# Paired attention of the second block: three pairs of score banks, one value product per pair of heads, and coefficients spread inside the steps

## The reference, cut to what matters

```python
def nsa_mixer(q, kc_raw, vc_raw, ks, vs, kw, vw, gates, ...):   # 8 heads of 64, 2 groups of keys and values
    # compressed keys:  o_c = softmax(q kc) vc
    # selected blocks:  the top 8 blocks of 64 keys; 512 tokens have 8 blocks, so all are taken
    s_s = q k_sel^T ; p_s = masked_softmax(s_s, causal) ; o_s = p_s v_sel
    # window of 512 keys: with 512 tokens this is again every key up to the token's own
    s_w = q k_win^T ; p_w = masked_softmax(s_w, causal) ; o_w = p_w v_win
    o = gates[0] * o_c + gates[1] * o_s + gates[2] * o_w
...
    return concatenate([o_a, o_b, o_c], axis=-1) @ w_out     # attention, pooling, gated linear attention
```

## Time and profile before

| what | us |
|---|---|
| median of 3 runs (3054.70 to 3055.62) | 3055.57 |
| the profiled execution, device time | 3055.25 |
| its span in the trace | 3053.4 |
| PE busy | 2989.9 |
| DVE busy | 1881.9 |
| ACT busy | 1284.5 |
| GpSimd busy | 1082.1 |
| attention of the second block, first layer, from the first turn to the first output product | 1558.21 to 1634.77 |
| the same, second layer | 2551.34 to 2627.90 |

### The profile page before, as it was taken

How to read it: one execution, slowest core, us unless ns; L and a number is a source line. 1 busy time by engine, 2 the same in 40 slices (tenths; PEclk the granted TensorE clock), 3 DMA queues, 4 the chain that set the end, 5 groups by cost and what they waited for, 6 DMA issues and landing times. The chain is left out here.

```text
span 3053.4 us, 43808 instructions
## 1 busy us (share of the span) xinstructions
PE 2989.9 (98%) x17636; PEld 2517.3 (82%) x17636; DVE 1881.9 (62%) x2718; ACT 1284.5 (42%) x2007; POOL 1082.1 (35%) x794
## 2 busy tenths in 40 slices
PE   8999999999999999999999999999999999999998
PEld 6887878788777789987867899978998776789996
DVE  7476244837524277854475777657785447577774
ACT  4356442436553243433473534324343347453432
POOL 2443445525354422325341332242232534133222
PEclk8999999999999999999999999999999999999999
DMA  6223315313231233222210233223322221033321
GB/s 272 100 84 110 100 43 200 138 59 111 97 104 53 83 114 104 94 90 80 81 42 29 104 104 104 97 76 114 104 95 89 77 83 42 29 104 104 104 97 49
DMA packets 57441, 287.63 MB, mean 94 GB/s; under 512 B 6776, under 2 KB 7288, under 8 KB 30200
## 3 DMA queue, kind: packets, MB, share of 16 engines
q1 hardware_dynamic: 54000, 269.30, 25.0%
q10 hardware_dynamic: 3240, 15.53, 1.6%
HBM read 282.64 MB, written 2.16 MB: 93 GB/s over the span
## 5 line engine op out<-in xcount | busy, mean ns | idle before, releaser
L152 POOL TENSOR_TENSOR w_parts<-w_raw,w_parts 128x512 fp32r<-128x512 f32 x376 | 535.7, 1456 | 717.3 <-ACT w_parts L141 691.9
L421 PE MATMUL PS<-x_parts,w_parts 128*128 128x512 f32 x2688 | 667.9, 394 | 1.6 <-ACT m_all L1424 1.6
L421 PEld LDWEIGHTS PS<-x_parts,w_parts 128*128 128x128 f32 x2688 | 500.5, 188 | 113.2 <-issue 9.6
L2169 POOL TENSOR_TENSOR partial_parts<-ffn_buffers,partial_parts 128x512 fp32r<-128x512 f32 x128 | 184.3, 1441 | 746.9 <-ACT partial_parts L2364 746.9
L2210 PE MATMUL PS<-hidden_parts,partial_parts 128*128 128x512 f32 x1536 | 372.7, 391 | 0.0
L2210 PEld LDWEIGHTS PS<-hidden_parts,partial_parts 128*128 128x128 f32 x1536 | 280.1, 188 | 53.4
L2190 PE MATMUL PS<-x_parts,w_parts 128*128 128x512 f32 x1152 | 264.8, 390 | 1.0 <-POOL x_parts L873 0.8
L2190 PEld LDWEIGHTS PS<-x_parts,w_parts 128*128 128x128 f32 x1152 | 215.3, 188 | 50.4 <-POOL x_parts L873 1.8
L141 ACT CAST w_parts<-w_raw 128x2048 fp32r<-128x2048 f32 (+1 forms) x92 | 170.6, 1855 | 158.8 <-PE PS L421 73.8
L2228 PE MATMUL PS<-x_combined_parts,w_parts 128*128 128x256 f32 x1536 | 204.2, 282 | 0.2
L2228 PE MATMUL PS<-x_parts,w_parts 128*128 128x256 f32 x1536 | 204.2, 282 | 0.0
(11 more groups left out here) (442 smaller groups left out, 5002.4 us busy)
## 6 DMA issues: line engine op xcount, KB each, us to landing
w_raw<-in_w_gu SPq DMA_DIRECT2D x88, 1024.0 KB, 4.8
w_raw<-in_w_in SPq DMA_DIRECT2D x70, 1024.0 KB, 4.9
ffn_buffers<-in_w_part SPq DMA_DIRECT2D x128, 256.0 KB, 2.7
w_raw<-in_w_out SPq DMA_DIRECT2D x24, 1024.0 KB, 4.8
m_all<-in_w_next SPq DMA_DIRECT2D x14, 1024.0 KB, 7.4
w_raw<-in_w_last SPq DMA_DIRECT2D x12, 768.0 KB, 4.2
m_all<-in_w_gate SPq DMA_DIRECT2D x8, 1024.0 KB, 4.8
ssd_buffers<-decay_rows ACTq DMA_DIRECT2D x16, 512.0 KB, 3.8
```

The lines of the kernel that those rows point to most:

```text
L152: pool.tensor_tensor(self.part(parts, u, 1, at, to), raw[:, self.slot(u), at:to], self.part(parts, u, 0, at, to).bitcast(F32), ALU.subtrac ...
L421: return pe.matmul(PS[0:m, self.bank(j), :], w[w_][:, k, c:c + m], part(x_, k), start=start, stop=stop)
L2169: pool.tensor_tensor(small_parts[:, d % 2, 1, :], small_raw[:, d % 2, :], small_parts[:, d % 2, 0, :].bitcast(F32), ALU.subtract).then_inc ...
```

## The change

The score of a step and its transposes now share a bank: step s uses banks 2(s % 3) and 2(s % 3) + 1, so three steps are under way in banks 0 to 5. turn(s, b) writes over the scores of step s, which DVE has read. score(s) therefore waits until both copies of step s - 3 are done, where it waited for the maximum of step s - 2. The PE list of a step becomes turn(s, 0), score(s + 2), `between(s)`, turn(s, 1), and after turn(3n + 3, 1) the weigh of the whole pair n. That weigh is eight products (four key tiles by two heads) with 512, 384, 256 and 128 columns instead of twenty with 128. The pt buffer holds a whole pair, laid out by key tile (`turned_tile`), so the copies of step 3n + 2 are two instructions each. Odd pairs' pt lies in the two slots of `RAW`; copy(3) waits until unit 11 has been split, and SP sends units 12 and 13 only after the last weigh.

Coefficients are computed per pair of heads in DVE's `after` of steps 2, 5, 8, ...; they are spread in `between` of steps 8, 10, 12, 14, 16, 19 and 22, all into bank 7, and scaled by DVE a step later. The finish of the gated linear attention is done in every second step from 0 to 14. Tiles 4 to 7 are rounded with pairs 1, 2, 3 and 5. The last pair's weigh and spread go into `proj.begin`, ahead of its n = 2; tiles 0 to 2 are rounded ahead of the last `take_output`.

```diff
             def begin(self, pe, jobs, x, order=range(KD), between=None):
                 for n in range(KD + 1):
+                    if between and n in between:
+                        between[n]()
...
+            def bank(self, s, b):
+                return 2 * (s % 3) + b
+            def turned_tile(self, s, b, i):
+                region = self.pt[s // 3 % 2][b]
+                return region[:, i * P:i * P + (i + 1) * 3 * P].rearrange("p (t c) -> p t c", c=3 * P)[:, :, 0:P]
+            def copy(self, eng, op, s, b):
+                eng.wait_ge(self.turned, 2 * s + b + 1)
+                if s == 3:
+                    eng.wait_ge(*self.lowered)
+                if s >= 6:
+                    eng.wait_ge(self.weighted, s // 3 - 1)
+                for _, i, at in self.tiles_of(s):
+                    last = op(self.turned_tile(s, b, i), split3(PS[:, self.bank(s, b), at:at + (i + 1) * P], i + 1))
+                last.then_inc(self.copied[b], 1)
...
             def score(self, pe, s):
-                if s >= 2:
-                    pe.wait_ge(self.smax, 2 * self.before(s - 1))
+                if s == 2:
+                    pe.wait_ge(self.emptied, 2)
+                for b in range(2):
+                    if s >= 3:
+                        pe.wait_ge(self.copied[b], s - 2)
...
-            def weigh(self, pe, s):
-                        for b in range(2):
-                            last = pe.matmul(PS[64 * b:64 * b + 64, 6, i * P:(i + 1) * P], self.vf(w, j // 2, t),
-                                             self.pt[:, s % 2, b, at + t * P:at + (t + 1) * P],
-                                             start=(t == 0), stop=(t == i))
+            def weigh(self, pe, n):
+                for t in range(NT):
+                    for b in range(2):
+                        at = (3 * t + t) * P
+                        last = pe.matmul(PS[64 * b:64 * b + 64, 6, t * P:T], self.vf(w, j // 2, t),
+                                         self.pt[n % 2][b][:, at:at + T - t * P],
+                                         start=(t == 0), stop=(t == NT - 1), skip_group_check=True)
...
                 for s in range(self.steps):
                     self.turn(pe, s, 0)
-                    self.turn(pe, s, 1)
                     if s + 2 < self.steps:
                         self.score(pe, s + 2)
-                    if s >= 1:
-                        self.weigh(pe, s - 1)
+                    between(s)
+                    self.turn(pe, s, 1)
+                    if s and s % 3 == 0:
+                        self.weigh(pe, s // 3 - 1)
                     after(s)
-                self.weigh(pe, self.steps - 1)
...
-                att.tensor(pe, after)
-                for j in range(4):
-                    spread_coefficients(1, j)
-                proj.begin(pe, (jo, jo + 1), parts, order)
+                def between(s):
+                    if s in SPREAD:
+                        spread_coefficients(SPREAD.index(s))
+                def last_pair():
+                    att.weigh(pe, last_n)
+                    spread_coefficients(last_n)
+                att.tensor(pe, between, after)
+                proj.begin(pe, (jo, jo + 1), parts, order, {2: last_pair})
...
                 def take_output(act, n):
-                    act.wait_ge(att.weighted, 3 * (n + 1))
+                    if n == last_n:
+                        for early in range(3):
+                            output_high(act, early)
+                    act.wait_ge(att.weighted, n + 1)
...
                 def after(s):
-                    if s < 8:
+                    if s in NORMED:
...
+                    if s % 3 == 2:
+                        coefficients(s // 3)
+                    if s - 1 in SPREAD:
+                        scale(SPREAD.index(s - 1))
...
                     n = len(stream.units)
+                    sp.wait_ge(att.weighted, att.steps // 3)
                     stream.send(sp, RAW, n)
```

More of the change, by code:

```diff
@@ L600, in score @@
                         r = slice(64 * b, 64 * b + 64)
-                        last = pe.matmul(PS[:, 2 * (s % 2) + b, at:at + n], self.q[r, j, i * P:(i + 1) * P],
+                        last = pe.matmul(PS[:, self.bank(s, b), at:at + n], self.q[r, j, i * P:(i + 1) * P],
                                          self.kd[r, w, j // 2, 0:n], start=True, stop=True)
@@ L607, in turn @@
                 pe.wait_ge(self.prob, 2 * self.before(s) + (b + 1) * n)
-                if s >= 1:
-                    pe.wait_ge(self.copied[b], s)
-                else:
-                    pe.wait_ge(self.emptied, b + 1)
                 for t in range(self.blocks(s)):
-                    last = pe.transpose(PS[:, 4 + b, t * P:(t + 1) * P],
+                    last = pe.transpose(PS[:, self.bank(s, b), t * P:(t + 1) * P],
                                         self.p[:, s % 2, b, t * P:(t + 1) * P], ident)
@@ L655, in scalar @@
             def scalar(self, act, take):
[L656 to L661, removed]
                 for s in range(self.steps):
@@ L665, in scalar @@
                         self.exponentials(act, s)
-                        copy(s - 1)
+                        self.copy(act, act.copy, s - 1, 1)
                     if s >= 2 and (s - 1) % 3 == 0:
                         take(act, (s - 1) // 3 - 1)
-                copy(self.steps - 1)
+                self.copy(act, act.copy, self.steps - 1, 1)
                 take(act, self.steps // 3 - 1)
@@ L680, in maximum @@
                             n = (i + 1) * P
-                            dve.tensor_tensor_reduce(self.p[:, s % 2, b, at:at + n], PS[:, 2 * (s % 2) + b, at:at + n],
+                            dve.tensor_tensor_reduce(self.p[:, s % 2, b, at:at + n], PS[:, self.bank(s, b), at:at + n],
                                                      const("causal")[:, T - n:T], -(HD ** -0.5), 3.0e38, ALU.add, ALU.min,
                                                      self.nm[:, 2 * tile + b:2 * tile + b + 1]).then_inc(self.smax, 1)
[L685 to L690, removed]
                 maximum(0)
@@ L695, in vector @@
                         maximum(s + 1)
-                    copy(s)
+                    self.copy(dve, dve.tensor_copy, s, 0)
                     after(s)
@@ L2702, in mix_tokens @@
                                   lambda w, g, t: v[:, t, w * P + g * HD:w * P + (g + 1) * HD],
-                                  (pair(0), pair(1), nm, None))
+                                  (pair(0), ((over[:, 4 * T:8 * T], pcs_and_turned),
+                                             (RAW[:, 0, :], RAW[:, 1, :])), nm, None))
             def row_sum(s, h):
@@ L3079, in take_output @@
                                        scale=p2("pool_s")[:, n:n + 1]).then_inc(s_pw, 1)
-                    if 0 < n < 5:
-                        if n == 2:
-                            act.wait_ge(s_fin, 8)
-                        act.wait_ge(s_pw, min(n, 2))
-                        k = order[n - 1]
+                    if n in MIXED:
+                        k = order[MIXED.index(n)]
+                        if k < 6:
+                            act.wait_ge(s_pw, k - 3)
+                        else:
+                            act.wait_ge(s_fin, NT * (k - 5))
                         act.copy(XS[:, 0, k, :], M[:, k, :]).then_inc(parts.high, 1)
                 att.scalar(act, take_output)
-                for j in range(4):
-                    act.wait_ge(s_oe, j + 1)
-                    act.copy(XS[:, 0, j, :], M[:, j, :]).then_inc(parts.high, 1)
+                output_high(act, 3)
             @block.vector
```

86 lines of the change are left out of this document (40 added, 46 removed).

## The result

The changed kernel takes 3061.42 us (median of 13 runs, 3059.25 to 3065.8), the kernel before 3055.62 on the same chip (13 runs, 3052.06 to 3059.07). The ratio is 1.0022, 95% interval 1.0015 to 1.0029: slower by 0.2%, some 6 us, where 6.6 were forecast. A second measurement later gave 1.0025 (1.0015 to 1.0035).

The account below looks back on a forecast made before the run. PE's instruction list plus its waits was taken to bound the kernel; -0.3 - 5.4 + 9.0 = +3.3 us a layer, +6.6 for two, gave 3062.2 us, between 3057 and 3067 (8 in 10: 3051 to 3069).

Parts of the forecast that it names:

- Part 1: PE's own work in a layer's attention: changes of form, long weigh products, moved spreads; -0.3 us a layer.
- changes of form: PE's one-time cost when the work's form switches; per pair 1.59 us before, 1.39 after, so -1.6 a layer.
- Part 2: PE's waits that go: turns no longer wait for bank 4 or 5 to be copied; -5.4 us a layer.
- turn groups: Twelve groups of a layer read as turns late for a bank's copy, 0.24 to 0.80 us each, 5.4 in all.
- Part 3: New PE waits: scores wait for ACT's copy of the preceding turn, some turns are late; +9.0 us a layer.
- The floor of 0.33: Score's least wait at steps 3n + 2: copy chain 0.80 us against PE's 0.33 + 0.15 of other work.
- Parts at nothing: Coefficients and scalings on DVE, last pair's weigh, early roundings, late units 12 and 13: no cost expected.
- The last pair's cover: Last weigh's wait for ACT's last copy, 0.8 us behind the turn, is covered by ten output products.
- Scores never stand: Rival: freed banks leave scores no wait; -5.7 us a layer, 3044 us; chance 0.12.
- floor alone: Rival: ACT's queue never delays the copy, only the bare chain counts; -0.6 us a layer, 3054.4; chance 0.18.
- Heads apart: Rival: the two heads' long weigh products run one behind the other; 17 us a layer more, 3096; chance 0.03.
- More standing: Rival: PE waits longer, through DVE's scalings or late unit 12; with 3 us a layer more, 3068; chance 0.09.

Follow-up runs that it names:

- the alternating run: Changed kernel with each pair's weigh cut into twenty 128-column products, the two heads alternating piece by piece: 3060.78 us, ratio 1.0011 to the kernel before.
- the copy between the heads: Changed kernel with ACT's copy of the step before placed between the exponentials of the two heads: 3057.11 us, ratio 1.0002 to the kernel before.
- the turns together: Changed kernel with the score put back behind both turns of its step: 3049.11 us, ratio 0.9986 to the kernel before.
- the turns together and the take late: Changed kernel with the score behind both turns and ACT's take of a pair one step later: 3046.21 us, ratio 0.9971 to the kernel before.

## Why the prediction came out right, step by step

The total was right (3062.2 against 3061.42), and so were the place and the releaser. But a layer's sum was +3.3 and the traces show +4.0; the medians hid that behind the scatter of the rest.

To part work from lateness I went through the intervals between the starts of neighbouring PE instructions in both traces, and set apart every one longer than an undisturbed one of its kind (0.109 between transposes, 0.203 from a last transpose to a score). The 0.03 to 0.06 more at nearly every crossing from one head's or step's transposes to the next, 1.4 a layer before and 1.8 after, stand there with or without a stop and count as work.

**Part 1, PE's own work, forecast -0.3.** Without the late intervals the stretches hold 82.3 us before and 81.8 after: -0.4. Heads side by side is right. Long products at -0.2 is right too: the alternating run puts them at 0.27 a layer. No run took the changes of form apart, so their terms are confirmed only in the sum.

**Part 2, late groups that go, forecast -5.4.** Ten turn groups of before are late by 0.21 to 0.78 (4.35 together), one turn behind a weigh by 0.33, one weigh by 0.48, and small ones make it 5.3. So the size is right, but one of the twelve "turn groups" (the 0.49 in the list) was no turn that waited for a bank. It was a weigh that waited for ACT's take:

```profile
1606.53 1.13 PE L601 MATMUL PS<-mixer_buffers 64*128 64x512 f32 x4
1608.08 1.09 PE L628 MATMUL PS<-mixer_buffers 128*64 128x128 f32 x16 [0.41 <-ACT mixer_buffers L3075]
```

**Part 3, what is late next, forecast +9.0.** By the same intervals: fifteen late scores, 8.4, and four late turns, 1.4, 9.8 in all. The forecast had the fifteen scores too, with 7.7, and 1.3 for turns. Step 1 is 0.68 (forecast 0.7). Four are 0.85 each, those of the steps 2, 5, 8 and 14, forecast at 0.74 or 0.75; this is the term that was mis-sized most, 0.4. The other ten lie between 0.35 and 0.55 and sum up to 4.3 (forecast 3 x 0.35 and 3.0). Of the turns, step 2 is 0.36 late, which the list left out; the steps 8 and 14 have 0.70 (0.87 forecast) and step 23 0.30 (0.4). The floor of 0.33 is in the rows exactly, and none of the six scores behind a weigh waits.

The errors of the parts are -0.1 (work), +0.1 (late groups) and +0.8 (waits), together the 0.7 between 3.3 and 4.0: nearly all of it lies in Part 3. The agreement of the total, to 0.8 us of 3062, owed something to scatter and doesn't vouch for the terms.

**Parts at nothing.** All held as far as the traces show. The output product starts 77.19 behind the first turn (76.6 forecast), is 14.40 long and PE busy for 14.40 of it; the change in it is 3.37 against 3.3. Units 12 and 13 came in time: L423 follows without idle time though the transfers now lie in this stretch (0.38 of the DMA engines, 147 GB/s, where the earlier trace rows had 27 GB/s earlier). The last pair's cover is worth 0.7 (0.8 forecast), with another engine's copy as the last one. No run took DVE's scalings apart; its finish in every second step is worth 0.96 a layer, which I had mentioned without a price.

**The rivals.** "Scores never stand" and "floor alone" fall by the fifteen rows; the copy between the heads shows what ACT's list held in them, 5.0 of 7.4. "Heads apart" falls by the 2.30. "More standing" was 3 a layer; there were 0.8.

## What to carry to other kernels

When a buffer's release moves in front of a short piece of work, write down the chain that releases it (engine's start after the signal, copy, signal back: 0.20 + 0.46 + 0.14 here) against what the waiting engine still has to do (0.48 here), and then look at what stands ahead of the copy in the copying engine's list; a waiting take in an engine with some 23 us a layer to spare cost PE 2.4 us a layer (measured with the turns together). The same freed banks, long products and spreads lost 4.0 us a layer with the score between the turns, and gained 4.4 with the turns together and the take late. For gains of some 0.1%, compare the stretch that was changed, in every layer: it repeats to 0.1 us where the rest of the program scatters by 3.

## What the runs showed of the hardware that I had not expected

Products on different halves of the array's columns ran fully side by side only where they alternated in the list: the same twenty products of a pair took 2.33 us with the heads alternating, and 2.82 with one to four pieces of a head in a row (the place of the flag that begins a sum differed as well; see that run). With long products each is followed by the other head's at once, which gives 2.30.
